# A begin of its own for every whole weight block, in 8-byte steps within 256 bytes

## The reference, cut to what matters

```
x = x + m[2] * rms_norm(mixer(modulate(rms_norm(x), m[0], m[1])))
x = x + m[5] * rms_norm(square(relu(h @ w1)) @ w2)      # h = modulate(rms_norm(x), m[3], m[4])
```

## Time and profile before

| what | value |
|---|---|
| median of the runs | 1960.72 us (1960.58 and 1960.86) |
| the profiled execution | 1961.04 us, of which 1959.2 us is the span of the trace |
| mean granted TensorE clock | 0.996 |
| TensorE matmuls | 10285, busy 1919.3 us (98%) |
| VectorE / ScalarE / GpSimd busy | 71% / 46% / 13% |
| DMA | 315.12 MB, mean 161 GB/s |

### The profile page before, as it was taken

How to read it: one execution, slowest core, us unless ns; L and a number is a source line. 1 busy time by engine, 2 the same in 40 slices (tenths; PEclk the granted TensorE clock), 3 DMA queues, 4 the chain that set the end, 5 groups by cost and what they waited for, 6 DMA issues and landing times.

```text
span 1959.2 us, 27475 instructions
## 1 busy us (share of the span) xinstructions
PE 1919.3 (98%) x10285; PEld 1607.6 (82%) x10285; DVE 1400.5 (71%) x2243; ACT 895.7 (46%) x1536; POOL 250.2 (13%) x332
## 2 busy tenths in 40 slices
PE   8999999999999999999999999999999999989998
PEld 4877788888888777889988888888888878878997
DVE  5898777888866655487997676767755567667765
ACT  3433355333343453576554224634233454557654
POOL 2101010211111200411101001101110021331000
PEclk9999999999999999999999999999999999999999
DMA  8434235655663451367875422655555245327763
GB/s 311 138 98 136 76 98 185 211 184 174 201 185 100 158 168 33 95 225 257 271 245 165 151 97 69 200 162 183 161 172 161 78 148 176 98 92 229 228 196 116
DMA packets 191827, 315.12 MB, mean 161 GB/s; under 512 B 14637, under 2 KB 114312, under 8 KB 191696
## 3 DMA queue, kind: packets, MB, share of 16 engines
q1 hardware_dynamic: 162512, 210.09, 33.0%
q0 software_dynamic: 29184, 103.29, 17.1%
HBM read 312.29 MB, written 1.05 MB: 160 GB/s over the span
## 4 chain that ended last, share of the span: by engine, by line
PE 82%; DVE 9%; issue 4%; ACT 2%; DMA 2%; POOL 1%; SPq 0%; DVEq 0%; POOLq 0%; ACTq 0%
PE bank L723 24%; PE bank L730 22%; PE bank L729 22%; PE bank L733 8%; DVE w L2242 3%; DVE acc L2267 2%; PE bank L728 2%; PE bank L726 2%; ACT junk L1642 1%; PE bank L785 1%; DMA raw<-in_mlp_w 1%; POOL st L3258 1%; PE bank L809 1%; DVE X L2386 1%; ACT w L1610 1%
## 5 line engine op out<-in xcount | busy, mean ns | idle before, releaser
L1610 ACT ACTIVATE w<-raw 128x1024 fp32r<-128x1024 f32 (+4 forms) x390 | 399.1, 1031 | 555.8 <-PE bank L730 481.8
L2242 DVE TENSOR_TENSOR w<-raw,w 128x1024 fp32r<-128x1024 f32 (+3 forms) x372 | 439.2, 1189 | 229.2 <-ACT w L1610 228.8
L723 PE MATMUL bank<-HH,w 128*128 128x256 f32 (+1 forms) x1552 | 509.5, 328 | 3.4 <-DVE HH L2369 2.0
L729 PE MATMUL bank<-HL,w 128*128 128x512 f32 (+1 forms) x1232 | 412.1, 334 | 0.0
L730 PE MATMUL bank<-HH,w 128*128 128x512 f32 (+1 forms) x1232 | 411.9, 334 | 0.0
L2267 DVE SCALAR_TENSOR_TENSOR acc<-ada,sc,acc 128x512 f32<-128x512 f32 x518 | 362.4, 746 | 2.3
L723 PEld LDWEIGHTS bank<-HH,w 128*128 128x128 f32 x1552 | 291.0, 188 | 30.5 <-issue 4.4
L723 PE MATMUL bank<-w,UH 128*128 128x512 f32 x768 | 300.7, 392 | 0.3 <-DVE UL L2544 0.3
L730 PE MATMUL bank<-w,UL 128*128 128x512 f32 x768 | 299.1, 390 | 0.0
L729 PE MATMUL bank<-w,UH 128*128 128x512 f32 x768 | 298.9, 389 | 0.0
L729 PEld LDWEIGHTS bank<-HL,w 128*128 128x128 f32 x1232 | 230.2, 187 | 26.1 <-issue 0.2
(11 more groups left out here) (354 smaller groups left out, 2610.1 us busy)
## 6 DMA issues: line engine op xcount, KB each, us to landing
raw<-in_mlp_w SPq DMA_DIRECT2D x256, 512.0 KB, 4.4
ada<-in_mod_w POOLq DMA_DIRECT2D x96, 512.0 KB, 4.5
ada<-in_ada_w POOLq DMA_DIRECT2D x80, 512.0 KB, 4.7
raw<-in_ml_w_qkvo SPq DMA_DIRECT2D x28, 512.0 KB, 3.7
raw<-in_conv_w_in SPq DMA_DIRECT2D x24, 512.0 KB, 4.2
raw<-in_ada_w SPq DMA_DIRECT2D x12, 512.0 KB, 6.1
raw<-in_mla_w_o SPq DMA_DIRECT2D x8, 512.0 KB, 3.9
raw<-in_gla_w_v SPq DMA_DIRECT2D x8, 512.0 KB, 4.0
```

Of the source, the lines that this page charges most:

```text
L723: pe.matmul(o, sh, mh, start=start, stop=False, skip_group_check=True)
L729: pe.matmul(o, sh, ml, start=False, stop=False, skip_group_check=True)
L1610: act.activation(k.halves(n)[0], k.raw[(NDIRECT + n) % NRAW][:, 0:m], ACT.Copy).then_inc(*k.w_hi.up("w hi", n))
L2242: dve.tensor_tensor(low, k.raw[(NDIRECT + n) % NRAW][:, 0:m], high.bitcast(F32), ALU.subtract).then_inc(*k.w_lo.up("w lo", n))
```

## The change

`begin` is no longer taken from `weight_stream`. Blocks are counted by kind. A kind is: narrow or not, in buffer `w0` or in one of the other four, and the shape. The k-th whole block of its kind (from 0) begins at element 2 * (k mod 32), that is 0, 8, 16, ... 248 bytes behind its buffer's start; in `w0`, where there is less room, at 2 * (k mod 8), 0 to 56 bytes. Blocks that are not whole begin at 0. The narrow blocks thus no longer stand at 8 bytes, but for one in 32 (one in 8 in `w0`). Of the whole blocks, 148 + 36 are of shape 2 x 512 (others + `w0`), 61 + 15 of shape 4 x 256 and not narrow, 83 + 21 narrow. The buffers grow by the room that the filler had, and the filler goes: 2048 + 62 elements are 8440 bytes where 8200 and 224 were before, so that the buffers and all else stay where they are. No instruction is added, removed or moved.

```diff
-        self.blocks, self.begin = zip(*weight_stream(A))
+        self.blocks, narrow = zip(*weight_stream(A))
+        self.begin, turn = [], {}
+        for n, block in enumerate(self.blocks):
+            kind = narrow[n], n % NSPL == 0, block.shape[1:]
+            turn[kind] = turn.get(kind, -1) + 1
+            whole = math.prod(block.shape[1:]) == 1024
+            self.begin.append(2 * (turn[kind] % (8 if n % NSPL == 0 else 32)) if whole and len(block.shape) == 3 else 0)
...
         for i in range(NSPL):
-            self.pair.append(sb(f"w{i}", [128, 2048 + NARROW_AT], F32R))
+            self.pair.append(sb(f"w{i}", [128, 2048 + (14 if i == 0 else 62)], F32R))
             if i == 0:
                 self.sc, self.minus_half = sb("sc", [128, 4, 8]), sb("minus_half", [128, 16])
-            sb(f"w_pad{i}", [128, 8 if i == 0 else 56])
```

## The result

The changed kernel takes 1991.02 us (1990.45 and 1991.59) against 1960.72 us before. The ratio is 1.0155, 95% interval 1.0111 to 1.0198: slower by about 30 us. The profiled execution has a span of 1988.6 us, 29.4 us more than before. The direction was forecast, and the time lies in the stated range, but the loss is twice the 14 us of the sum.

The account below looks back on a forecast made before the run. TensorE was taken to bound the kernel; 12.4 us (512 columns) + 3.1 (256 columns) - 1.5 (absorbed) = 14.0 us on 1961.0 gave 1975.0, stated as 1975 us, 0.7% slower, range 1950 to 2001 us.

Parts of the forecast that it names:

- What bounds the kernel: TensorE, 82% of the chain; same instructions in the same order, so only how long an instruction takes can alter.
- 512-column products: TensorE's 5232 products over whole blocks: spacing from 226.7 to 229.2 ns, 12.4 us more after 5% off.
- 256-column products: TensorE's 2784 products with the block stationary: 1.1 ns more each, 3.1 us.
- Re-settling: TensorE streams at each of 364 blocks: some five products at about 5 ns, counted inside the 2.5 ns per 512-column product.
- Writers of the blocks: ScalarE's copy and VectorE's difference writing at the new begins: taken as zero.
- Absorbed: Slower TensorE products in stretches that wait for a block or vector step cost nothing: a tenth off, 1.5 us.
- A: Rival on TensorE's spacing: any offset settles at the same spacing, nothing changes; 1956 to 1966 us, chance 0.20.
- B: Rival on 512-column products: equal starts may be worst, others save 4.3 ns each, 22 us; 1939 us, chance 0.14.
- C: Rival on off-unit block starts: one more access each, moving ones costing most; slower by over 2%, 2012 us, chance 0.14.
- The rule of the Trainium skill: TensorE's two read ports are independent and never wait, so begins have no consequence: sum zero, 1961 us.
- The signs: Trace marks for the forecast: 512-column mean 228 to 231 ns, begin 0 at 226.7, 256-column 115 to 120, writers and clock unchanged.

Follow-up runs that it names:

- e9: Changed kernel with 8 begins (0 to 56 bytes) instead of 32, a new one for every block of a kind: 1991.71 us, 1.0163 against the kernel before.
- e10: Changed kernel with 8 begins (0 to 56 bytes), each held for 16 blocks in a row: 1992.53 us, 1.0166 against the kernel before.
- e7: Kernel before with narrow blocks beginning 88 bytes on instead of 8: 1959.39 us, 0.9990 against the kernel before.
- e1: Changed kernel with spread begins only for 2 x 512 blocks, others as in the kernel before: 1977.01 us, 1.0082 against the kernel before.
- e2: Changed kernel with spread begins only for four-row-tile blocks, 2 x 512 blocks at 0: 1974.02 us, 1.0065 against the kernel before.
- e4: Kernel before with blocks and activations all moved on by 8 bytes, relations kept: 1989.55 us, 1.0140 against the kernel before.
- e8: Kernel before with blocks and activations all moved on by 16 bytes, relations kept: 1987.87 us, 1.0139 against the kernel before.
- e5: Kernel before with a 32-byte filler ahead of HH shifting everything behind it, relations kept: 1962.41 us, 1.0003 against the kernel before.
- e3: Changed kernel with every whole block beginning at 8 bytes, no spread: 1983.80 us, 1.0111 against the kernel before.

## Why the prediction was right or wrong

**What bounds the kernel: right.** TensorE's spacing moved; counts, clock and the other engines' durations are the same.

**512-column products: the mis-sized term, 12.4 us forecast.** I took 229.2 ns, close to the 228.9 ns of the earlier trace rows and about halfway between the settled 226.7 and the unsettled 232, "since with many different offsets some streams will settle and others won't". They measured 232.6 (moving) and 231.9 (stationary), 18.7 + 8.9 = 27.6 us. The reading behind the number was wrong: that a stream settles doesn't mean that it settles at the fast rate. With begins other than 0 streams settle too, but nearly always at a slow rate, most often 233.3; only 4 of 219 stretches are at 226.7. The 232 ns after an interruption, which I held for a passing state and an upper bound, was the better estimate of an arbitrary placement. With it the term would have been 5232 x 5.3 = 27.7 us. The stream over 64-column tiles, to which I leaned, has other loads.

**256-column products: right in sign, mis-sized.** 1.1 ns taken, 2.5 measured, 7.0 us instead of 3.1. The mean of the begins, 118.2 ns, lies more than halfway to the 120 ns of the earlier trace rows, and I went a quarter of the way.

**Re-settling: wrong.** I counted it as part of the loss. e9 and e10, with some 380 and 24 changes of begin, are 0.8 us apart and the wrong way round: it adds nothing that the runs resolve.

**Writers of the blocks: right**, 1057 and 1223 ns.

**Absorbed: right in kind, low in size.** I took off a tenth. The sum of 34.6 us became 29.4 in the span, 15%. One place can be seen when the two traces are set side by side by the number of the matmul: the changed kernel falls back by 0.4 to 2.8 us per 500 matmuls from the 1500th on, but between the 5000th and the 5500th (982 to 1055 us in the kernel before) it loses nothing. This is layer 1's feed-forward. Before, window 850 to 1070, and after, window 860 to 1083:

```profile
850.00:1070.00 220.00, 217.60 (x1437) 199.05 (x1438) 190.97 (x280) 128.18 (x211) 25.10 (x37) 0.99 0.72 236
```

```profile
860.00:1083.00 223.00, 222.39 (x1443) 202.33 (x1444) 191.46 (x279) 127.79 (x209) 25.51 (x37) 0.99 0.73 234
```

The columns are length, busy of PE, PEld, DVE, ACT and POOL, clock, DMA share and GB/s. TensorE's idle time shrank from 2.4 to 0.6 us, with VectorE at 87% and DMA at 72%. The chain of the kernel before, cut to this window:

```profile
by line: DVE w L2242 16.7%; PE bank L723 12.3%; DVE acc L2267 10.2%; issue 8.4%; DMA raw<-in_mlp_w 7.2%; PE bank L730 6.6%; PE bank L729 6.6%; PE bank L728 5.7%; PE bank L726 5.5%; DMA ada<-in_mod_w 3.4%; ACT w L1610 2.3%; DVE UL L2544 2.2%
```

TensorE's lines in it hold 37% of the window, against 82% over the whole span; after the change they hold 97% of the same stretch. So VectorE and the loads set the pace in much of it before, and the slower products used up their slack. This is where the chain lost much of VectorE's share. That e7's 4.5 us arrive as 1.9 fits it, but no run isolates that.

**The rivals.** A (nothing changes) and B (faster) are out; B's guess that equal starts are the worst nearly holds for 256 columns (119.8 ns, the worst of the table 120.2) and is the reverse of the truth for 512. C (over 2%) didn't happen, and its mark, 5 ns between moving and stationary blocks, neither: they differ by 0.7 ns. The rule of the Trainium skill (SBUF — State Buffer, Who interferes with whom), by which TensorE's two read ports are independent and wait on nobody, would make the sum zero; e1, e2, e4 and e8 contradict that: 13 to 28 us from begins alone. It is the place of one operand relative to the other that counts, not only its own: a moving block at 32 bytes stands at 233.3 ns beside a stationary operand at 0, and moving blocks at 32 beside a stationary operand at 32 (e5) stand at 227.1 ns on average.

**The signs.** Held: the clock, the writers' durations, and the blocks at begin 0, which settle at 226.7 ns. Missed: the mean of the 512-column products was to be 228 to 231 ns and is 231.9 to 232.6; the 256-column streams were to lie between 115 and 120 ns, and some are at 113.3. The time lies in the range because the range was 51 us wide; the sum was short by half.

## What to carry to other kernels

In a kernel that TensorE bounds with back-to-back float32r products of 512 columns, let stationary and moving operands start on 32 bytes and equal modulo 256 bytes. Here nearly every other begin cost 0.7 to 3.6% of the spacing (the table and the sentence behind it), and begins off this rule for all blocks cost 1.1 to 1.7% of the time. Products of 256 columns have a best begin of their own (88 or 8 bytes off here, not 0), so measure it per shape. A spread of begins over blocks in one run is a cheap table of them: read the spacing per block from the trace, then make the best one uniform. Take several blocks per begin, since one begin can show two rates.

## What the runs showed of the hardware that I had not expected

A stream's spacing depends on its begins, and for many of them it is reproduced in every kernel: 230.7 ns for a stationary block at 8 bytes in the changed kernel, in e2 and in e3. Several settled values are multiples of 6.67 ns, the time in which 512 columns at 213.3 ns stream 16 of them, that is 64 bytes: 113.3 is 17 of these, 120.0 is 18, 226.7 is 34, 233.3 is 35. In the kernel before, the starts of the settled 512-column streams between 380 and 1600 us also fall on one such grid throughout (it drifts by 1.6 ns per 1000 us), though interruptions lie between them. That speaks for reads that are served on a fixed grid of time, but no run here isolates it, and why 120 bytes works as a stationary begin, and why 256 columns prefer 8 or 88 bytes to 0, stays open. Some begins have two settled rates (64 bytes at 256 columns: 113.3 or 117.8 ns in different streams; 240 bytes, moving, at 512 columns: 226.7 or 236.7 ns for one and the same block). So the begin alone doesn't fix the rate: how a stream enters a block has a part in it, and what chooses wasn't found.
